# Slot weights on ScalarE, one sum for expert numbers, stick values by whole steps, sliding heads in pairs: one change to a one-core hybrid encoder with product-key experts

## What is computed

```
z = (q @ k) * 64**-0.5                                  # stick-breaking branch, 8 heads x 64
log_keep = where(k_pos < q_pos, -softplus(z), 0)
weight = exp(log_sigmoid(z) + reverse_cumsum(log_keep) - log_keep)
o_sb = weight @ v
...
o_sw = softmax over a 3-chunk window with ALiBi and a sink; 8 query heads, 2 key/value heads x 64
o_mem = softmax(q @ mk) @ mv                            # 4 heads x 128, 256 memory tokens
x += (sum_b sigmoid(gate_b) * (o_b @ w_o_b)) @ w_out
...
s = keys @ q                                            # PEER: 8 heads, two halves of 128 keys
v1, i1 = top_k(s[:, :, 0], 16);  v2, i2 = top_k(s[:, :, 1], 16)
best, flat = top_k(v1[:, None] + v2[None, :], 16)
idx = i1[flat // 16] * 128 + i2[flat % 16]
a = gelu(u_tab[idx] . x)
x += sum_k softmax(best)_k * a_k * v_tab[idx_k]
```

## Time and profile before

| | us |
|---|---|
| median of 3 runs | 4567.03 |
| lowest to highest | 4560.62 to 4580.06 |
| the profiled execution, its own time | 4562.79 |
| its span, first to last instruction | 4561.0 |

### The profile page before, as it was taken

The page is one execution under the profiler, slowest core; times in us unless marked ns, Lnnn a source line. Parts: engine busy times, 40 slices in busy tenths (PEclk is TensorE's granted clock), DMA queues, the critical chain, the costliest instruction groups (busy, mean ns, idle before and its releaser), DMA issues.

```text
span 4561.0 us, 34579 instructions
## 1 busy us (share of the span) xinstructions
PE 3581.2 (79%) x10561; PEld 1891.6 (41%) x10561; DVE 2945.0 (65%) x6134; ACT 1507.8 (33%) x2980; POOL 2015.6 (44%) x1542
## 2 busy tenths in 40 slices
PE   7997689876676699888487767799886677777777
PEld 4544355642333444554243444444553233233222
DVE  2130321298997788679699766687679677677554
ACT  2110420135675432233377643223232211111111
POOL 0000000055555577666666545577665533333332
PEclk9998799987788899999688876799998899999999
DMA  4313213499787699999998878899998999999998
GB/s 165 116 58 108 79 56 103 170 358 369 268 320 315 243 408 401 421 420 373 391 346 325 312 288 311 332 395 421 416 421 323 389 420 417 415 415 417 421 421 356
DMA packets 269915, 1448.47 MB, mean 318 GB/s; under 512 B 28432, under 2 KB 70160, under 8 KB 116112
## 3 DMA queue, kind: packets, MB, share of 16 engines
q0 software_dynamic: 165888, 1208.03, 65.9%
q1 hardware_dynamic: 103840, 238.22, 14.3%
HBM read 1400.93 MB, written 46.14 MB: 317 GB/s over the span
## 4 chain that ended last, share of the span: by engine, by line
POOL 36%; issue 23%; PE 13%; DMA 11%; DVE 5%; ACT 2%; POOLq 0%; SPq 0%; DVEq 0%; ACTq 0%
POOL side L1028 20%; POOL ring L1017 16%; DMA ring<-in_experts_dram,idx 11%; PE ps L1299 5%; PE ps L1226 3%; DVE ring L1707 2%; PE ps L1232 1%; PE ps L1247 1%; ACT diag L1436 1%; PE ps L1270 1%; PE ps L1185 0%; PE ps L1151 0%; POOLq L1027 0%; PE ps L1083 0%; DVE hot L1488 0%
## 5 line engine op out<-in xcount | busy, mean ns | idle before, releaser
L1017 POOL DMA_INDIRECT ring<-in_experts_dram,idx x1152 | 1110.1, 964 | 2509.3 <-PE ps L1299 1449.2
L1299 PE MATMUL ps<-ring,diag 128*128 128x512 f32 x3072 | 1625.9, 670 | 664.8 <-ACT diag L1436 640.4
L1707 DVE CUSTOM_DVE_ANT_0 ring<-ring,ps 128x1024 f32<-128x1024 f32 x1152 | 1380.1, 1218 | 580.2 <-DMA ring<-in_experts_dram,idx 562.0
L1299 PEld LDWEIGHTS ps<-ring,diag 128*128 128x128 f32 x3072 | 611.0, 210 | 1500.4 <-ACT diag L1436 871.2
L1028 POOL TENSOR_TENSOR side<-side,ring 128x1024 f32<-128x1024 f32 x384 | 905.0, 2357 | 8.2
L1448 ACT ACTIVATE act_<-hid 128x2 f32<-128x2 f32 x576 | 117.0, 203 | 1918.8 <-DVE hid L1707 1908.5
L1441 ACT ACTIVATE ring<-ring,wgt 128x1024 f32<-128x1024 f32 x384 | 435.2, 1133 | 0.0
L1226 PE MATMUL ps<-work 128*128 128x384 f32 x1152 | 392.2, 489 | 0.8 <-issue 0.8
L1682 DVE TENSOR_TENSOR wgt<-act_,gw 128x2 f32<-128x2 f32 x576 | 370.2, 643 | 8.6 <-ACT act_ L1448 8.6
L1436 ACT ACTIVATE diag<-const,wgt 128x128 f32<-128x128 f32 x768 | 281.5, 389 | 201.8 <-DVE wgt L1682 199.7
L1226 PEld LDWEIGHTS ps<-work 128*128 128x128 f32 x1152 | 221.2, 192 | 173.1 <-issue 40.6
(11 more groups left out here) (177 smaller groups left out, 3382.6 us busy)
## 6 DMA issues: line engine op xcount, KB each, us to landing
work<-in_w_gate_o_dram SPq DMA_DIRECT2D x72, 768.0 KB
work<-in_w_q_dram SPq DMA_DIRECT2D x24, 1024.0 KB
ring<-in_experts_dram,idx POOLq DMA_INDIRECT x1152
work<-in_w_out_dram SPq DMA_DIRECT2D x12, 1024.0 KB
w_qkv<-in_w_in_dram SPq DMA_DIRECT2D x5, 2048.0 KB, 9.8
work<-k_scratch SPq DMA_DIRECT2D x37, 256.0 KB, 5.5
work<-v_scratch SPq DMA_DIRECT2D x37, 256.0 KB
o_x<-q_scratch SPq DMA_DIRECT2D x9, 768.0 KB, 10.0
```

The costliest lines, as they stand in the source:

```text
L1017: i = nc.gpsimd.indirect_dma_start(out=ring[:, j % RING, :], out_offset=None, in_=A["experts"], in_offset=bass.IndirectOffsetOnAxis(ap=idx ...
L1299: last = nc.tensor.matmul(acc[:, h, :], diag[:, (by_pe(j) - 1) % 4, :], ring[:, j % RING, DM + h * HB:DM + (h + 1) * HB], start=(j % SLOTS ...
L1707: last = nc.vector.tensor_tensor_reduce(out=u, in0=u, in1=xp, scale=1.0, scalar=0.0, op0=ALU.mult, op1=ALU.add, accum_out=hid[:, j % SLOTS ...
```

## The change

1. **Slot weights.** `product` on VectorE goes. ScalarE makes `wgt` itself: for each of the two slots a copy of `act_` scaled by `gw` (128x1 each). The one-batch delay of `spread` goes too: gelu, weights, diagonal matrix and ring scaling of batch Q stand together, ahead of the front steps of iteration Q. TensorE's order stays.
2. **Expert numbers.** The product with the key numbers becomes two instructions of 128x256, the first also times 128, and one sum over both tables writes `idx`. `e12` and L1494 go.
3. **Stick values.** Both halves of a step come at tau b + 6: eight matmuls whose output alternates between the two halves of the array's columns. `pv` counts steps. The waits on it, and the reload of the value buffer on SP, are put in steps.
4. **Sliding heads.** Unit c = 0 or 1 now has two query heads of each of the two key/value heads. Scores alternate between the row halves, values between the column halves, and the copy out is 128x256. ALiBi slopes and sinks are put in the new order on the host.

Core of the diff:

```diff
-        self.zscore, self.soft, self.suffix, self.values = at(0), at(1), at(2), at(6)
+        self.zscore, self.soft, self.suffix = at(0), at(1), at(2)
+        self.values = {x[5] + 6: k for k, x in enumerate(self.steps_)}
...
+                        for b in range(1 if kb is not None else DB):
+                            c = slice(b * DS, (b + 1) * DS) if kb is None else slice(0, P)
+                            for h in range(2 * 4):
+                                j, p = h // 2, h % 2
+                                val = vcache[:, b, h * HD:(h + 1) * HD] if kb is None else vbuf[:, at % 3, h * HD:(h + 1) * HD]
+                                w = wts[:, f.half(k, p) % 5, j * P:(j + 1) * P]
+                                last = nc.tensor.matmul(ps[p * HD:(p + 1) * HD, 7, j * P:(j + 1) * P][:, c], val, w[:, c],
+                                                        start=first and j == 0, stop=end, skip_group_check=True)
...
-                        r = slice((c % 2) * HD, (c % 2 + 1) * HD)
-                        for j in range(4):
+                        for s4 in (0, 2, 1, 3):
+                            gg, j = s4 // 2, 2 * c + s4 % 2
+                            r = slice(gg * HD, (gg + 1) * HD)
...
+                            for jj in range(2):
+                                for kk in range(2):
+                                    for gg in range(2):
+                                        last = nc.tensor.matmul(ps[rows[gg], 7, (2 * c + jj) * P:(2 * c + jj + 1) * P], vsw[:, i + kk, rows[gg]], probs(2 * gg + jj, kk),
+                                                                start=(kk == 0), stop=(kk == 1), skip_group_check=True)
...
                         if x >= 5:
-                            act.wait_ge(pv, x - 4)
+                            act.wait_ge(pv, (x - 5) // 2 + 1)
...
-                if Q:
-                    spread((Q - 1) // NB, (Q - 1) % NB)
-                if Q < NT * NB:
-                    advance(1 + Q)
+                    act.wait_ge(gelus, m * NB + q + 1)
+                    for i in range(q * BATCH, (q + 1) * BATCH):
+                        last = nc.scalar.activation(wgt[:, i:i + 1], act_[:, i:i + 1], ACT.Copy, scale=gw[:, m % 2, i:i + 1])
+                    last.then_inc(weights, 1)
+                    act.wait_ge(weights, m * NB + q + 1)
...
+                    advance(1 + m * NB + q)
...
-                link(nc.vector.tensor_tensor(hot[:, :, :, :], hot[:, :, :, :],
-                                             i16f[:, :, :].unsqueeze(2).to_broadcast([P, 2, TOPK, TOPK]), ALU.mult))
-                link(nc.vector.tensor_reduce(e12[:, :, :].rearrange("p a k -> p (a k)"), hot[:, :, :, :].rearrange("p a k i -> p (a k) i"), AX, ALU.add))
-                link(nc.vector.scalar_tensor_tensor(out=idx[:, m % 2, h * TOPK:(h + 1) * TOPK], in0=e12[:, 0, :], scalar=float(NK), in1=e12[:, 1, :],
-                                                    op0=ALU.mult, op1=ALU.add))
+                for a in range(2):
+                    last = nc.vector.scalar_tensor_tensor(out=hot[:, a], in0=hot[:, a], scalar=float(NK if a == 0 else 1), in1=i16f[:, a].unsqueeze(1).to_broadcast([P, TOPK, TOPK]),
+                                                          op0=ALU.mult, op1=ALU.mult)
+                link(last)
+                with nc.allow_low_precision(reason="whole numbers below 16384 summed in float32, written as uint32"):
+                    link(nc.vector.tensor_reduce(idx[:, m % 2, h * TOPK:(h + 1) * TOPK], hot[:, :, :, :].rearrange("p a k i -> p k a i"), AXY, ALU.add))
...
-            def product(Q):
-                m, q = Q // NB, Q % NB
-                dve.wait_ge(gelus, Q + 1)
-                c = slice(q * BATCH, (q + 1) * BATCH)
-                nc.vector.tensor_tensor(wgt[:, c], act_[:, c], gw[:, m % 2, c], ALU.mult).then_inc(weights, 1)
```

More of the change, by code:

```diff
@@ L60, in host_constants @@
     mask_s = ((k // DS == q // DS) & (k < q)).astype(float)
-    slopes = 2.0 ** (-8.0 * np.arange(1, SWH + 1) / SWH)
+    order = [g * GRP + 2 * c + jj for c in range(2) for g in range(KVH) for jj in range(2)]
+    slopes = (2.0 ** (-8.0 * np.arange(1, SWH + 1) / SWH))[order]
     qn, kn = i[:, None], np.arange(2 * P)[None, :]
@@ L900, in front @@
                     if tau in f.values:
-                        k, p = f.values[tau]
-                        if p == 1 and k + 3 < f.nkeys:
-                            sp.wait_ge(pv, f.half(k, 1) + 1)
+                        k = f.values[tau]
+                        if k + 3 < f.nkeys:
+                            sp.wait_ge(pv, f.half(k, 0) // 2 + 1)
                             load_v(f, k + 3)
@@ L1427, in _ @@
             advance(0)
-            def spread(m, q):
-                act.wait_ge(weights, m * NB + q + 1)
-                for j in range(m * SLOTS + q * BATCH, m * SLOTS + (q + 1) * BATCH):
-                    if sided(j):
-                        continue
-                    d = by_pe(j) - 1
-                    if d >= 4:
-                        act.wait_ge(pe_done, d - 3)
-                    last = nc.scalar.activation(diag[:, d % 4, :], ident, ACT.Copy, scale=wgt[:, j % SLOTS:j % SLOTS + 1])
-                last.then_inc(diags, 1)
-                for j in range(m * SLOTS + q * BATCH, m * SLOTS + (q + 1) * BATCH):
-                    if sided(j):
-                        v = ring[:, j % RING, DM:2 * DM]
-                        nc.scalar.activation(v, v, ACT.Copy, scale=wgt[:, j % SLOTS:j % SLOTS + 1]).then_inc(scaled, 1)
@@ L1709, in _ @@
                     last.then_inc(dots, 1)
-                    if m or q:
-                        product(m * NB + q - 1)
                     c = q - TOP_FROM[m]
@@ L1724, in _ @@
                     advance(1 + m * NB + q)
-            product(NT * NB - 1)
             finish(ST)
@@ L1798 @@
     A["cache_mem_kT"] = give("cache_mem_kT", _np.asarray(inputs["cache_mem_k"][0]).transpose(0, 3, 2, 1).reshape(DB, P, MH * MT))
+    order = [g * GRP + 2 * c + jj for c in range(2) for g in range(KVH) for jj in range(2)]
+    A["sinks"] = give("sinks", _np.asarray(inputs["sinks"])[:, order])
     small, wide = host_constants()
```

103 lines of the change are left out of this document (55 added, 48 removed).

## The result

| | before | after |
|---|---|---|
| median, us | 4567.37 | 4416.8 |
| lowest to highest, us | 4560.62 to 4580.06 | 4411.57 to 4423.65 |
| span of the profiled execution, us | 4561.0 | 4409.8 |
| first gather starts at, us | 896.1 | 881.7 |
| last dots of tile 5 end at, us | 3572.2 | 3426.2 |

The ratio is 0.9668, with a 95% interval of 0.9641 to 0.9695: 151 us less. The forecast was 4430, so it was right in sign and 13 us off in size.

The account below looks back on a forecast made before the run. VectorE's own work was taken to bound three expert-loop stretches, DMA the others. 133 - 15 + 9 + 3 + 8 = 138 us less than the profiled 4562.8 gave 4425, predicted as 4430 us; range 4340 to 4540.

Parts of the forecast that it names:

- the three stretches: Expert loop at 912 to 1596, 2052 to 2964 and 3420 to 3572 us; DMA engines idle 272 us, the gain's cap.
- the missing delay: Diagonal matrices no longer wait for the next batch's dots: 9 us at tile ends, 3 us at the kernel's end.
- VectorE's relief: In the three stretches: 137 us off VectorE for weights, 25 for expert numbers, 162 in all; 133 on the path.
- ScalarE's charge: In the three stretches: 15 us lost to ScalarE's new scaled copies, mainly at 2280 to 2508 us; ends 0 and 30.
- The 60% of standing that vanishes: Of VectorE's standing in the three stretches, 167 us in slot weights and 39 in expert numbers, 60% goes.
- the DMA-bound stretches: 1596 to 2052 and 2964 to 3420 us, DMA engines always busy at 413 GB/s; rows free earlier are worth nothing.
- The ring is full and VectorE is late: In the three stretches VectorE's own work is the limit, since it waits only 227.8 us for gathers in 2660 us.
- (a): Rival: in the three stretches VectorE's standing only moves to other instructions, 39 us saved, 32 on the path; 4530 us; 14%.
- (b): Rival: all of VectorE's standing vanishes, 245 us saved, 201 on the path; 4346 us; 10%.
- (c): Rival: slower, ScalarE's order becomes the limit in tiles 0 to 5; 4634 us; 6%.
- (d): Rival: the ring, not VectorE, limits the three stretches; only ends and front gain, 20 us; 4547 us; 7%.
- Group 0's front: The front that nothing hides: TensorE's shorter sliding scores and values save 8 us, with 0 and 15 as ends.

Follow-up runs that it names:

- the weights alone: The kernel before with only part 1: slot weights made on ScalarE and the one-batch delay dropped; 4475.2 us.
- Delay kept: The changed kernel with the one-batch delay put back on ScalarE for weights, diagonal matrices and ring scaling; 4476.2 us.
- one-source product: The kernel before with VectorE's slot-weight product as two 128x1 products by a per-partition scalar; 4516.7 us.
- one sum only: The kernel before with only part 2: two 128x256 products and one sum that writes the expert numbers; 4535.7 us.
- with parts 2 to 4: The kernel before with parts 2 to 4, slot weights as two 128x1 per-partition-scalar products on VectorE, and the one-batch delay; 4447.7 us.
- doubling the copies: The changed kernel with each 128x1 scaled copy on ScalarE made twice, the extra result read by nobody; 4442.2 us.
- the ring of eight: The changed kernel with RING = 8 instead of 10, so gathers run one batch less ahead; 4539.6 us.

## Why the prediction was right

**The total was right; it came out of errors that cancel, so that it is as close as 13 us is luck.** In the three stretches the sum said 133 - 15 = 118 us less, and 115 was measured. But 52.5 of the 115 come from the missing delay, to which the sum gave nothing there; VectorE's relief less ScalarE's charge brought 62.5.

**VectorE's relief in instruction time: right.** 162 us were expected, 169 measured (1426.7 to 1257.4). By part it was less even: 119 for 137 with the weights alone, 31 for 25 with the numbers alone, and the rest only with all parts together. The 60% of standing that vanishes was 69% by the excess of durations. Part 2 was worth 31 instead of 20 to the time, since its products hardly stand.

**Its share of the path and ScalarE's charge: together 48 us too hopeful.** The steps are "with VectorE 82% busy, about that share is on the path" and "I charge 15 us for this in all". Delay kept has both and not the missing delay: in the three stretches VectorE is busy for 532.2 + 631.1 + 110.7 = 1274 us, 153 less, which at 82% less 15 us would be 110 us; the time is 62.5 less, 41%. How much of the gap is which stays open. Three runs leave ScalarE alone: they give 62 of 91 us (one-source product), 25 of 31 (one sum only) and 76 of 111 (with parts 2 to 4, in an execution 16 us over its median, so that it may be over 80%). So two thirds to four fifths of the relief reached the time: 82% was somewhat high at most. By these shares the 153 us would be 104 to 125, and 62.5 were measured: 42 to 63 us for ScalarE, an estimate, where I had charged 15 with 30 as the end. But doubling the copies adds only 24 us in the three stretches of after, for less work than the first pair, so a part of the gap may be relief that brings less the more of it there is. The row of waits, 352 us against 228, says where the relief went that did not reach the time: VectorE stood for rows not yet back.

**The missing delay: mis-sized by a factor of five.** 12 us were expected, all at tile and kernel ends; it is 59. This is the term that made up for the last. The end of the kernel did as expected: 2.8 us, and the last chain now closes with eight passes (start us, us, what), where the earlier trace rows had sixteen:

```profile
4401.77 3.71 PE ps L1303 x8
```

What I had dismissed is the middle. "The ring is full and VectorE is late" was read off a wait of 227.8 us, but in the same 2660 us GpSimd stood 249 times for TensorE and VectorE 148 times for a gather: a full ring and a waiting VectorE take turns within a stretch. GpSimd's 860.3 us of waiting for TensorE's sums was the row to follow: between 880 and 3430 us it was 816.9 and is 714.8 now. I had also put the gain in the DMA-bound stretches at nothing; 16.7 us came, 10 of them with the delay.

**Rivals.** (a) and (b) fall with the 69%, and the time is 113 us under (a)'s and 71 over (b)'s. (c) falls by the doubled copies. (d), the ring as the limit, was half right and had the wrong conclusion. I let it give 20 us only, as if rows came back no earlier. In truth the same change returns them 3.3 us earlier, half a batch, and the ring of eight shows what 4.6 us of lead are worth: 123 us.

**Group 0's front: 14.4 us instead of 8**, inside its range of 0 to 15. (In all runs the first gather starts at 896.1 to 899.4 us with the old front and at 881.4 to 886.9 with the new one.) TensorE in the front of group 0 of after (start us, duration us, idle before):

```profile
528.83 1.97 PE L1110 MATMUL ps<-work 128*64 128x128 f32 x32
531.96 1.14 PE L1149 MATMUL ps<-work,o_x 64*128 64x256 f32 x8 [1.17 <-DVE work L1538]
539.00 2.08 PE L1149 MATMUL ps<-work,o_x 64*128 64x256 f32 x8 [5.90 <-ACT work L1366]
...
562.45 2.07 PE L1149 MATMUL ps<-work,o_x 64*128 64x256 f32 x8 [2.81 <-ACT work L1366]
```

The sliding scores take 2.08 and 2.07 us, from 3.78 and 2.99. The first unit, which waits for only 1.2 us, takes 1.14 from 1.96 at a granted clock of 1.00 and 0.97: near the 1.1 I had named. I had undersized the values. They halve too, 1.96 to 1.09 us for 16 passes, and both lie in one chain: its steps start 1.5 us earlier at 532 us, 4.0 at 547, 6.5 at 562 and 10.0 at 583.

## What to carry over

When two engines feed each other through a ring, ask of every change by how much earlier or later a row comes back, and measure it by making the ring one batch shorter: here that alone, 4.6 us less lead, cost 123 of the 151 us that were won. What an engine's relief is worth beside such a ring has to be measured too: two thirds to four fifths of VectorE's came through where nothing else changed, and less than half where ScalarE took over the work. Who does a tiny operation matters less than whose order it has to pass through, and a two-input product that stands beside GpSimd can be rewritten with a per-partition scalar before it is moved to another engine.

## What the runs showed of the hardware

- A 128x1 product on VectorE with a per-partition scalar took at most 215 ns in the 334 cases that began while a 2.36 us GpSimd add was under way. The 128x2 product with two SBUF inputs took 0.157 us in tiles 6 to 8, and stood in 155 of 159 such cases, 2.68 us in the one of the earlier trace rows.
- Standing moves along VectorE's order: the 128x256 sum behind the product began while an add was under way in none of 55 cases before, and in 33 of 55 once the product no longer stood.
- A one-input 128x16 uint32 instruction stands as well: 973 ns on the mean in after, 175 in tiles 6 to 8.
- A 128x1 scaled copy on ScalarE takes 287 ns; two in a row keep it busy for 0.48 us together, four for 0.37 us more.
- Alternating the halves of the array pass by pass took 8 sliding scores from 1.96 to 1.14 us and 16 values from 1.96 to 1.09 us.
